# First stage of a diffusion-trunk kernel: six weight slots instead of four, x loaded first, a new order of units

## The reference

```python
m = jax.nn.silu(cvec) @ w_mod + b_mod          # for c and for c_ctx; w_mod is 2048 x 12288
sh1, sc1, g1, sh2, sc2, g2 = jnp.split(m, 6, axis=-1)
h = rmsnorm(x, g_pre1) * (1 + sc1) + sh1       # 640 tokens x 2048
proj = h @ w_in                                # the values are 1024 of its 9216 columns
```

## Time and profile before

| | us |
|---|---|
| median of 3 runs (2847.01 to 2848.12) | 2847.84 |
| the profiled execution | 2848.99 |
| its span, first to last instruction | 2847.4 |
| TensorE busy in the span | 2791.4 |
| VectorE, ScalarE, GpSimd busy | 2106.8, 1502.7, 282.0 |
| mean granted TensorE clock | 0.993 of full speed |

### The profile page before, as it was taken

How to read it: one execution, slowest core, us unless ns; L and a number is a source line. 1 busy time by engine, 2 the same in 40 slices (tenths; PEclk the granted TensorE clock), 3 DMA queues, 4 the chain that set the end, 5 groups by cost and what they waited for, 6 DMA issues and landing times.

```text
span 2847.4 us, 40931 instructions
## 1 busy us (share of the span) xinstructions
PE 2791.4 (98%) x15008; PEld 2390.7 (84%) x15008; DVE 2106.8 (74%) x1918; ACT 1502.7 (53%) x1466; POOL 282.0 (10%) x337
## 2 busy tenths in 40 slices
PE   7999999999999999999999997999999999999998
PEld 5688888899999999999988776888888888888886
DVE  2339788796777777763344577888888888888888
ACT  4411221125556566552233455777777777777776
POOL 1000000002111111100000001001010101100100
PEclk9999999999999999999999997999999999999999
DMA  9877667664343443364343767999999999999997
GB/s 370 311 266 255 228 252 265 224 227 135 120 123 119 123 123 123 102 207 124 123 143 119 292 215 276 356 402 395 395 398 389 396 393 397 391 388 387 392 394 297
DMA packets 258406, 757.23 MB, mean 266 GB/s; under 512 B 20249, under 2 KB 127297, under 8 KB 194001
## 3 DMA queue, kind: packets, MB, share of 16 engines
q1 hardware_dynamic: 234272, 650.01, 61.3%
q0 software_dynamic: 23120, 100.71, 10.9%
q10 hardware_dynamic: 928, 5.33, 0.5%
HBM read 700.61 MB, written 55.37 MB: 265 GB/s over the span
## 4 chain that ended last, share of the span: by engine, by line
PE 91%; DVE 3%; DMA 2%; ACT 1%; issue 1%; DVEq 0%; ACTq 0%; SPq 0%; POOL 0%; POOLq 0%
PE ps L542 21%; PE ps L544 21%; PE ps L543 21%; PE ps L2402 5%; PE ps L2403 5%; PE ps L2404 5%; PE ps L2569 3%; PE ps L2571 3%; PE ps L2570 3%; PE ps L2259 2%; PE ps L2507 1%; DMA raw<-in_w_mod 1%; DVE rsd L1827 1%; PE ps L2282 1%; DVE xc L1649 0%
## 5 line engine op out<-in xcount | busy, mean ns | idle before, releaser
L467 DVE TENSOR_TENSOR we_lo<-raw,we_hi 128x2048 fp32r<-128x2048 f32 x384 | 877.5, 2290 | 114.0 <-ACT we_hi L462 113.8
L462 ACT ACTIVATE we_hi<-raw 128x2048 fp32r<-128x2048 f32 x384 | 736.9, 1920 | 261.4 <-PE ps L544 261.4
L411 ACT ACTIVATE w_hi<-raw 128x2048 fp32r<-128x2048 f32 x115 | 220.1, 1914 | 444.3 <-PE ps L544 356.5
L421 DVE TENSOR_TENSOR w_lo<-raw,w_hi 128x2048 fp32r<-128x2048 f32 x115 | 263.5, 2291 | 192.4 <-ACT w_hi L411 187.8
L542 PE MATMUL ps<-we_hi,xs_lo 128*128 128x512 f32 x1024 | 399.7, 390 | 0.1
L544 PE MATMUL ps<-we_hi,xs_hi 128*128 128x512 f32 x1024 | 399.3, 390 | 0.0
L543 PE MATMUL ps<-we_lo,xs_hi 128*128 128x512 f32 x1024 | 399.3, 390 | 0.0
L2402 PE MATMUL ps<-hi,w_lo 128*128 128x320 f32 x1152 | 365.3, 317 | 0.9 <-ACT stage L1122 0.9
L2403 PE MATMUL ps<-lo,w_hi 128*128 128x320 f32 x1152 | 355.9, 309 | 0.0
L2404 PE MATMUL ps<-hi,w_hi 128*128 128x320 f32 x1152 | 355.8, 309 | 0.0
L1614 DVE SCALAR_TENSOR_TENSOR mod_acc<-mod_raw,sc,mod_acc 128x2048 f32<-128x2048 f32 x120 | 276.7, 2348 | 3.3
(11 more groups left out here) (447 smaller groups left out, 4772.0 us busy)
## 6 DMA issues: line engine op xcount, KB each, us to landing
raw<-in_w_e_gate SPq DMA_DIRECT2D x128, 1024.0 KB, 8.0
raw<-in_w_e_up SPq DMA_DIRECT2D x128, 1024.0 KB, 7.5
raw<-in_w_e_down SPq DMA_DIRECT2D x128, 1024.0 KB, 12.1
raw<-in_w_in SPq DMA_DIRECT2D x144, 512.0 KB, 5.7
mod_raw<-in_w_mod SPq DMA_DIRECT2D x64, 1024.0 KB, 5.3
raw<-in_w_mod SPq DMA_DIRECT2D x64, 512.0 KB, 7.6
raw<-in_w_o SPq DMA_DIRECT2D x64, 512.0 KB, 4.9
d_proj<-g_stage POOLq DMA_DIRECT2D x32, 320.0 KB, 2.4
```

The lines of the kernel that those rows point to most:

```text
L411: act.activation(w_hi[:, j % NHL, s], raw[:, slot, s], ACT.Copy).then_inc(hi_ready, 1 if fine else 2)
L421: dve.tensor_tensor(w_lo[:, j % NHL, s], raw[:, slot, s], w_hi[:, j % NHL, s].bitcast(F32), ALU.subtract).then_inc(lo_ready, 1 if fine else 2)
L462: act.activation(we_hi[:, k % NEH, :], raw_slot(k), ACT.Copy).then_inc(hi_ready, 2)
L467: TTn(we_lo[:, k % NEH, :], raw_slot(k), we_hi[:, k % NEH, :].bitcast(F32), ALU.subtract).then_inc(lo_ready, 2)
```

## The change

- **Six slots.** `NFIRST` is 6: units go to slot i mod 6. Slots 0 to 3 are those of `raw`, slots 4 and 5 the second and third tile of `mod_raw`. Unit i now waits for unit i - 6. The diagonals move to an area called `spare`. Counts of the loading semaphores follow (`loads_ahead`).
- **x first.** SyncE loads the five x tiles ahead of all weights, each with a semaphore of its own; three of these are shared with later uses, whose counts are raised by 16. ScalarE no longer loads x, and touches its Sqrt table before the first square.
- **Order of the units.** The value units stand at indices 6, 13, 20 and 27 of `START`, before at 8, 13, 22 and 31.
- **TensorE's order.** The turn of x0 is the first work; the other turns stand between modulation units 0 to 5. Units and value tiles alternate in another pattern, with some value tiles adjacent (0 and 1; 8, 9 and 10). The row turns 3, 5 and 7, which stood inside `first_values` 3, 7 and 11, stand between other steps: 3 after unit 16, 5 after k=6, 7 after k=11.
- **ScalarE's and VectorE's order.** ScalarE takes x0 after the third square; VectorE takes all x tiles before it copies the turned parameters, which now lie in bank 3. The split of value unit 0 on VectorE stands between and behind the two `mod_columns`.

```diff
+NFIRST = 6
-QUADS = [8, 2, 8, 8, 4, 8, NE * 6]
+QUADS = [5, 2, 8, 8, 4, 8, NE * 6]
...
-START = [("mod", m) for m in range(8)] + [("v", 0)] + [x for h in range(1, 4) for x in [
-    ("mod", 8 * h + m) for m in range(4)] + [("v", h)] + [("mod", 8 * h + m) for m in range(4, 8)]]
+V_PLACE = (6, 13, 20, 27)
+_mods = iter(range(32))
+START = [("v", V_PLACE.index(i)) if i in V_PLACE else ("mod", next(_mods)) for i in range(36)]
...
+        def first_slot(i):
+
+            j = i % NFIRST
+            return raw[:, j, :] if j < NRAW else mod_raw[:, j - NRAW + 1, :]
+
         def start_loaded(eng, i):
 
-            eng.wait_ge(raw_loaded[i % NRAW], (i // NRAW + 1) * INC)
+            eng.wait_ge(raw_loaded[i % NFIRST], (i // NFIRST + 1) * INC)
...
-                if i >= NRAW:
-                    what, n = START[i - NRAW]
+                if i >= NFIRST:
+                    what, n = START[i - NFIRST]
...
+            for t in range(TT):
+                src = a["x_sample"][0][t * P:(t + 1) * P, :] if t < TT - 1 else a["x_prompt"][0]
+                sp.dma_start(x_in[:, t, :], src).then_inc(x_sems[t], 16)
...
+            act.activation(misc[:, 6:7], eps_col, ACT.Sqrt)
...
-            load_x(0)
-            load_x(1)
             for t in range(TT):
                 square(t)
-                if t + 2 < TT:
-                    load_x(t + 2)
-                if t:
-                    take_x(t - 1)
+                if t >= 2:
+                    take_x(t - 2)
+            take_x(TT - 2)
+            take_x(TT - 1)
             row_out(0)
             v_split_hi(act, 0, 0)
             row_out(1)
             v_split_hi(act, 0, 1)
-            take_x(TT - 1)
...
             for t in range(TT):
                 norm_diagonal(t)
                 if t:
                     take_x(t - 1)
+            take_x(TT - 1)
+            dve.wait_ge(S["rows_turned"], 2)
+            own.done(dve.tensor_copy(A["cols_b"][:], ps[:, 3, 0:48]))
+            own.done(dve.tensor_copy(A["cols2"][:], ps[:, 3, 64:169]))
+            own.settle()
+            mod_columns(0)
             v_split_lo(dve, 0, 0)
-            mod_columns(0)
+            mod_columns(1)
             v_split_lo(dve, 0, 1)
-            take_x(TT - 1)
-            mod_columns(1)
...
             pe.wait_ge(S["c_ready"], 1)
+            turn_x(0)
             mod_unit(0)
+            turn_x(1)
             mod_unit(1)
+            turn_x(2)
+            mod_unit(2)
+            mod_unit(3)
+            turn_x(3)
             turn_parameters()
-            for m in range(2, 8):
-                mod_unit(m)
-                if m == 7:
-                    turn_rows(0)
-                if m >= 3:
-                    turn_x(m - 3)
+            mod_unit(4)
+            turn_x(4)
+            mod_unit(5)
+            mod_unit(6)
+            turn_rows(0)
+            mod_unit(7)
+            pe.wait_ge(S["xt_act"], 2 * TT)
+            pe.wait_ge(S["xt_dve"], 2 * TT)
+            mod_unit(8)
             turn_rows(1)
...
-            mod_units(8, 11)
+            mod_units(9, 11)
             first_values(0)
+            first_values(1)
             mod_units(11, 12)
-            first_values(1)
-            mod_units(12, 13)
             first_values(2)
+            mod_units(12, 14)
             turn_rows(2)
-            mod_units(13, 16)
-            first_values(3, amid=3)
-            mod_units(16, 18)
+            mod_units(14, 16)
+            first_values(3)
+            mod_units(16, 17)
+            turn_rows(3)
+            mod_units(17, 18)
             first_values(4)
-            mod_units(18, 20)
+            mod_units(18, 21)
             first_values(5)
-            mod_units(20, 21)
+            mod_units(21, 22)
+            turn_rows(4)
+            mod_units(22, 24)
             first_values(6)
-            turn_rows(4)
-            mod_units(21, 24)
-            first_values(7, amid=5)
-            mod_units(24, 26)
+            turn_rows(5)
+            first_values(7)
+            mod_units(24, 27)
             first_values(8)
-            mod_units(26, 28)
             first_values(9)
-            mod_units(28, 30)
             first_values(10)
+            mod_units(27, 30)
             turn_rows(6)
             mod_units(30, 32)
-            first_values(11, amid=7)
+            first_values(11)
+            turn_rows(7)
             for k in range(12, KT):
                 first_values(k)
```

More of the change, by code:

```diff
@@ L66 @@
 MOD_FROM = [sum(MOD_TILES[:n]) for n in range(8)]
-START = [("mod", m) for m in range(8)] + [("v", 0)] + [x for h in range(1, 4) for x in [
-    ("mod", 8 * h + m) for m in range(4)] + [("v", h)] + [("mod", 8 * h + m) for m in range(4, 8)]]
+V_PLACE = (6, 13, 20, 27)
+_mods = iter(range(32))
+START = [("v", V_PLACE.index(i)) if i in V_PLACE else ("mod", next(_mods)) for i in range(36)]
 MOD_AT = {m: i for i, (what, m) in enumerate(START) if what == "mod"}
 V_AT = {m: i for i, (what, m) in enumerate(START) if what == "v"}
-assert all(i % NRAW == m for m, i in V_AT.items()) and len(START) == (Q_V + 1) * NRAW
+assert all(i % NFIRST == m for m, i in V_AT.items()) and len(START) == (Q_V + 1) * NFIRST
 ORDER = (4, 2, 3, 0, 1)
@@ L184, in trunk @@
         sel2 = at("sel2", [P, 2], F32, mod_at + KT * 32 * 4)
-        A["diag"] = at("diag", [P, 2, P], F32, mod_at + 2 * UB + 256)
+        A["diag"] = at("diag", [P, 2, P], F32, PLACED["spare"])
         mod_acc = at("mod_acc", [P, 2, D], F32, s0 + 15360)
@@ L370, in trunk @@
                  "gates_hi": ("row_act", 8), "gates_lo": ("small_dve", 2)}
+        x_sems = x_loaded + [S["g2_loaded"], S["vec_lat_loaded"], S["rope_loaded"]]
         for name, (early, _) in LATER.items():
@@ L434, in f_loaded @@
             j = (F_UNIT + t) % NSLOT
-            return raw_loaded[j], (Q_EXP * INC if j < NRAW else 0) + (UNITS // NSLOT * NE + 1) * 16
+            return raw_loaded[j], loads_ahead(j) + (UNITS // NSLOT * NE + 1) * 16
         def unit_left(eng, k):
@@ L446, in exp_loads @@
         def exp_loads(e, k):
-            return (Q_EXP * INC if k % NSLOT < NRAW else 0) + (UNITS // NSLOT * e + k // NSLOT + 1) * 16
+            return loads_ahead(k % NSLOT) + (UNITS // NSLOT * e + k // NSLOT + 1) * 16
         def by_block(x):
@@ L471, in unit_wait, with loads_ahead @@
             pe.wait_ge(lo_ready, 2 * NRAW + 2 * (quad * NRAW + j + 1))
+        def first_slot(i):
+            j = i % NFIRST
+            return raw[:, j, :] if j < NRAW else mod_raw[:, j - NRAW + 1, :]
         def start_loaded(eng, i):
-            eng.wait_ge(raw_loaded[i % NRAW], (i // NRAW + 1) * INC)
+            eng.wait_ge(raw_loaded[i % NFIRST], (i // NFIRST + 1) * INC)
+        def loads_ahead(j):
+            return Q_EXP * INC if j < NRAW else (Q_V + 1) * INC if j < NFIRST else 0
         def v_split_hi(act, kq, p):
@@ L570, in wide @@
             def wide(w, j, kq, c0):
-                v = raw[:, j, :].rearrange("p (k n) -> p k n", k=4)
+                v = first_slot(j).rearrange("p (k n) -> p k n", k=4)
                 return [(v[:, 2 * i:2 * i + 2, :],
@@ L1012, in _ @@
             act.sem_inc(hi_ready, 2 * Q_V * NRAW)
-            def load_x(t):
-                src = a["x_sample"][0][t * P:(t + 1) * P, :] if t < TT - 1 else a["x_prompt"][0]
-                act.dma_start(x_in[:, t, :], src).then_inc(x_loaded[t % 2], 16)
+            act.activation(misc[:, 6:7], eps_col, ACT.Sqrt)
             def square(t):
-                act.wait_ge(x_loaded[t % 2], (t // 2 + 1) * 16)
+                act.wait_ge(x_sems[t], 16)
                 own.settle()
@@ L1517, in tokens @@
                 TTn(lo[:, k, :], xT[:, k, :], hi[:, k, :].bitcast(F32), ALU.subtract).then_inc(S["tok_lo"], 1)
[L1519 to L1522, removed]
             for t in range(TT):
@@ L1696, in head @@
                 split_lo(dve, Q_GATE + h, 1)
-                dve.wait_ge(S["rope_loaded"], 16)
+                dve.wait_ge(S["rope_loaded"], 32)
                 def rotate(i, x, turned, loaded, dst):
@@ L2055, in _ @@
                 if c == 0:
-                    dve.wait_ge(S["vec_lat_loaded"], 32)
+                    dve.wait_ge(S["vec_lat_loaded"], 48)
                 if c == 2:
@@ L2215, in _ @@
             expert(NE - 1, 1, True)
-            dve.wait_ge(S["g2_loaded"], 32)
+            dve.wait_ge(S["g2_loaded"], 48)
             def gain(i, t):
@@ L2282, in mod_unit @@
                     last = pe.matmul(ps[32 * kk:32 * kk + 32, bank, :], c2[:, 4 * kp + kk, :],
-                                     raw[:, i % NRAW, kk * 512:kk * 512 + 512], start=(kp == 0), stop=(kp == 3))
+                                     first_slot(i)[:, kk * 512:kk * 512 + 512], start=(kp == 0), stop=(kp == 3))
                 last.then_inc(S["start_used"], 1)
@@ L2300, in turn_parameters @@
                 pe.wait_ge(par_loaded, N_PAR * 16)
-                turn(ps[:, 4, 0:48], A["rows3"][:], 48)
```

(7 more changed lines are left out.)

6 lines of the change are left out of this document (2 added, 4 removed).

## The result

| | before | after |
|---|---|---|
| median, us | 2847.98 (2847.01 to 2850.27, 10 runs) | 2857.99 (2854.06 to 2861.40, 10 runs) |
| profiled execution, us | 2848.99 | 2861.40 |
| its span, us | 2847.4 | 2859.8 |

The ratio is 1.0034, with an interval of 1.0026 to 1.0042: the change makes the kernel 10.0 us slower. I had forecast 2849.7 and a range up to 2854.0; the result lies 8.3 us above the one and 4.0 above the other. The runs of after also lie farther apart, 7.3 us against 3.3, and the slower ones had the lower mean granted clock: four at 0.994 or 0.995 took 2854.1 to 2856.6 us, six at 0.991 to 0.993 took 2857.2 to 2861.4.

What follows compares the result with a forecast made beforehand. TensorE and the DMA loads were both taken as nearly full, stage delays reaching the end one for one. Start, chains and load waits made k=12 1.9 us late: 2847.84 + 1.9 = 2849.7 us, range 2845.0 to 2854.0.

Steps and rivals of the forecast that it cites:

- The start: Up to value tile k=0: unit 0 lands at 20.6, k=0 starts at 51.3, before 51.64, a gain of 0.3 us.
- The starved identity: Small loads beside x rows land late at the start; k=0 up to 5.8 us late, 2853.9 us in all; chance 0.08.
- The open token chains: Moved row turns 3 and 7 leave TensorE gaps of 2.4 us before k=4 and 3.4 us before k=12.
- The landing dates from unit 15 on: Weight loads land evenly, one MiB every 2.71 us, counted from index 11 at 50.4 us.
- Value units 2 and 3: Their splits free load slots: the first done about 85 us, hidden by 2 us, the second at 107.9.
- The third hole: Load queue dry until the split of value unit 3 ends at 107.9; unit 31 lands at 118.3, 0.2 us waited.
- The clock: Rival: TensorE's clock falls in the new gaps, 1.8 to 3.3 us a fall, likely 2851.5 to 2853.0; chance 0.18.
- signs of being wrong: Units landing before they are wanted, k=0 starting ahead of 50, or a granted clock of 0.50 after 30 us.
- two falls at the high price: Two clock falls in TensorE's gaps, each at the 3.3 us of all 6.6 us at half rate: 2856.3 us.
- my floor: With no load waited for, TensorE's steps and token chains put k=12 at 121.8, 3.3 us ahead.

Runs made afterwards that it cites:

- e7: Kernel before with six slots and the new places of the value units, ScalarE loading x and all orders as before: 2853.55 us.
- e1: Changed kernel with row turns 3 and 7 put back inside value tiles 3 and 11: 2853.01 us.
- e2: Changed kernel with VectorE splitting both halves of value unit 0 ahead of the second mod_columns: 2854.96 us.
- e12: e9 with fifteen dummy turns of the identity on TensorE, four ahead of unit 9 and eleven ahead of unit 10: 2847.05 us.
- e6: Changed kernel with the edits of e1, e2 and e5 together: 2849.66 us.
- e11: Changed kernel with only TensorE's steps from unit 11 on put back into the order of before: 2852.68 us.
- e9: Changed kernel with TensorE's order of before from unit 11 on, value unit 0 split earlier on ScalarE and VectorE, value units 2 and 3 split earlier: 2846.15 us.
- e3: Changed kernel with dummy turns of the identity on TensorE in four gaps, before unit 15, k=4, unit 31 and k=12: 2853.64 us.
- e4: Changed kernel with four slots and the old places of the value units: 2874.83 us.
- e10: e9 with four slots and the old places of the value units: 2853.37 us.
- e8: Kernel before with x loaded first by SyncE and the Sqrt table touched early, four slots, old orders: 2855.07 us.
- e5: Changed kernel with the splits of value units 2 and 3 moved behind the second token tile of the group before, on ScalarE and VectorE: 2855.48 us.

## Why the prediction was wrong, step by step

**The start: right.** Unit 0 was to end TensorE's wait at 20.6 and came at 20.52; unit 10 landed at 50.67 (50.4), k=0 at 51.66 (51.3). The first turn of x came at 15.36 and not at 13.7, and took 5.23 and not 4.65, without effect, since unit 0 was to be waited for anyway. The starved identity did not happen: 1.8 us more, inside the 2.2 that were free. It took 7.9 to 8.2 us to land in every run with x first, and 6.3 and 5.7 in before and e7. The rule that the Trainium skill has for it (DMA: Bandwidth & Descriptors, Queues, rings and completion order), that each DMA engine goes round the queues packet by packet, had the direction right; no run isolates it.

**The open token chains: right.** 2.41 and 3.41, where I had 2.4 and 3.4. e1 takes the first away and brings the second to 1.21.

**The landing dates from unit 15 on: wrong, the first step that failed.** I did not date the split of value unit 0, behind whose slot every later load waits, and let all units behind it land at an even 2.71 us, so unit 15 at 66.7. In after the split ended at 49.02, SyncE issued nothing from 42.9 to 49.04, and unit 15 came at 69.99. Its second half is held by both engines: on VectorE it stood behind the second `mod_columns`, which waited 2.33 us for the row turn behind unit 8, and on ScalarE behind `row_out(1)`. That is why e2, which moves VectorE's half alone, left the hole open. Where both are moved the hole is closed, and unit 15 is there by 67.4 (e12); in the runs with the hole it landed between 68.2 (e6) and 70.4 (e1). With all splits moved and TensorE's order held, 6.5 us come back (e11 to e9).

**Value units 2 and 3: right, but late with the rest.** I had the split of the first "done about 85", that of the second at 107.9. They ended at 89.36 and 112.86, 4.4 and 5.0 late, and k=4 and k=8, whose token chains they follow, were 4.9 and 5.0 late. So the second hole is an echo of the first and of the clock: where the split ended at 86.7 or before (e3, e1, e11) it is not there. The third hole was forecast, but what follows it was sized too small: from the end of the split to the landing of unit 31 I had 10.4 us (some 5, then twice 2.7), and it took 11.8, in e2 too. So the wait for unit 31 was 1.57 and not 0.2.

**The clock: a rival at 0.18, and it happened three times.** A granted clock of 0.50 behind 30 us was one of my signs of being wrong. I had priced two falls at the high price at 2856.3. The step that failed is the condition: "the open chains make gaps of 2.4 and 3.4" counted gaps of the token chains alone. Two of the falls came in waits for loads that I had not foreseen, 2.73 and 1.57 us; the third came in the 3.41.

**The sum.** In the profiled execution the forecast amounts to 2850.9 and was missed by 10.5. The rows give 0.4 at k=0, 2.7 for unit 15, 1.4 for unit 31 and 7.1 of half clock, 11.6 together, so something behind k=12 gave back 1.1. In the medians the miss is 8.3 us. e3, at full clock, takes 2853.6: by it **some 4 of the 8.3 us are the clock and some 4 the loads**. This is a rough division, since e3 differs from after by 4.35 with intervals of more than 2 us on either side, and its loads came a little earlier too.

**Where the expected gain went.** The two slots, with the places of the value units, are worth 16.8 us in the new orders (e4) and 7.2 in those of e9 (e10), so they do what they are for. They pay for x: to load it first costs 6.9 alone (e8), since 5 MiB pass before the first weights, and with the old orders this is not won back. With x loaded by ScalarE and the orders of before, the slots win nothing (e7): unit 6 comes 2.9 us later, and nothing is gained behind it. That the change could bring at best the difference of two things of 7 us is my reading of these runs, and no run shows that the two add up. e9 comes to 2846.15, 2.15 below before; my floor "if no load were waited for", k=12 at 121.8, was not reached: the earliest, e12, had k=12 at 123.69 with 1.7 us of waits for loads between 70 and 100 us and 1.2 for tokens.

**What remains open.** Whether e9 is truly faster than before: its interval ends at 1.0002. What made unit 15 land anywhere from 68.2 to 70.4 behind much the same hole. What decides whether the clock falls in a gap of 1.6 or 2.4 us.

## What to carry to other kernels

A load list worked in strict order is only as deep as its slowest release: with more slots, date the release of every slot, those freed by another engine's queue above all. If the release needs two engines, as a split does here, moving it on one of them changed nothing (e2); look at the next issue in the trace to see that an edit did what it was for. A gap has two prices, its length and the clock behind it; dummy work in the gap tells which of the two one pays. And before a cold stretch or a wait is removed, ask what sets the pace behind it; if it is the bytes, nothing is gained.

## What the runs showed of the hardware that I had not expected

- A gap need not be long for the clock to fall. The gap of 3.41 before k=12 brought a fall, in it or up to 1.1 us behind its end, in all four traces that have it unfilled (after, e2, e4, e5). That of 2.41 or 2.42 before k=4 did in e2 and e4 and not in after and e5. Gaps of 1.5 to 1.65 did at 124.2 in after, at 50.0 in e1 and at 49.7 in e9, and left the clock at 1.00 in many other places.
- One program can fall in one execution and not in another. after and e1 are the same program up to k=3, and both wait 1.6 us for unit 10. The clock stayed at 1.00 in after and fell in e1, although TensorE was a little less busy from 46 to 50 us in after (2.54 us of 4, against 2.66).
- Issuing becomes slow when much is in flight, and not by the slots alone. The longest issue of a 512 KB weight load by SyncE took 7.9 to 8.2 us where the five x tiles were issued ahead of it, with four slots (e4, e8, e10) as with six (after, e9); it took 5.8 us with six slots and x from ScalarE (e7), and 1.65 us before. SyncE did not need the time here.
- A deep queue moves bytes at the same 387 GB/s as a shallow one between holes. It makes them later instead: 10.6 to 11.3 us from issue to landing in the median in the traces with six slots, and 7.0 to 7.4 with four (before, e4, e8, e10).
